# Loading and releasing an expert's up matrices by halves of the contraction

## The reference

```python
# t: 512 x 1024; w_up1, w_up3: 32 x 1024 x 512; w_down: 32 x 512 x 1024
y = jnp.zeros_like(t)
for e in range(N_EXPERTS):                      # 32
    hid = jax.nn.silu(t @ w_up1[e]) * (t @ w_up3[e])
    y = y + combine[:, e:e + 1] * (hid @ w_down[e])
```

## Time and profile before

| what | value |
|---|---|
| median of 3 runs | 1287.11 us (1286.87 to 1289.26) |
| profiled execution | 1290.17 us |
| its span, first to last instruction | 1288.4 us |
| mean granted TensorE clock | 0.937 |
| TensorE busy | 1077.4 us, 84% of the span |
| weight loads of TensorE | 558.0 us |
| VectorE / ScalarE / GpSimd busy | 348.6 / 266.6 / 193.5 us |
| read from memory | 275.56 MB |
| SP's transfer queue | 263.33 MB, 52.8% of 16 engines' span |

### The profile page before, as it was taken

How to read it: one execution, slowest core, us unless ns; L and a number is a source line. 1 busy time by engine, 2 the same in 40 slices (tenths; PEclk the granted TensorE clock), 3 DMA queues, 4 the chain that set the end, 5 groups by cost and what they waited for, 6 DMA issues and landing times.

```text
span 1288.4 us, 15070 instructions
## 1 busy us (share of the span) xinstructions
PE 1077.4 (84%) x6355; PEld 558.0 (43%) x6355; DVE 348.6 (27%) x544; ACT 266.6 (21%) x406; POOL 193.5 (15%) x238
## 2 busy tenths in 40 slices
PE   0599999979999999999899469987878888887870
PEld 0578544545556677554345323333323333332320
DVE  3722562155547211102423421000000000000004
ACT  2233340255432343113112100000000000000003
POOL 2435100033330001000100011211111111111000
PEclk9799999989999999999999679989999999988895
DMA  9413103214431002214150849999999999999945
GB/s 307 174 66 131 65 3 128 65 66 164 163 135 63 2 2 68 99 34 149 47 212 33 330 181 406 403 396 400 410 404 409 406 413 402 381 396 408 411 176 199
DMA packets 69388, 280.49 MB, mean 218 GB/s; under 512 B 8379, under 2 KB 17709, under 8 KB 61147
## 3 DMA queue, kind: packets, MB, share of 16 engines
q1 hardware_dynamic: 59232, 263.33, 52.8%
q0 software_dynamic: 5120, 8.40, 2.0%
q10 hardware_dynamic: 4986, 8.04, 1.8%
HBM read 275.56 MB, written 12.58 MB: 224 GB/s over the span
## 4 chain that ended last, share of the span: by engine, by line
PE 50%; DMA 29%; DVE 12%; SPq 5%; ACT 2%; issue 1%; POOL 0%; ACTq 0%; POOLq 0%; DVEq 0%
DMA arena<-in_w_up 23%; PE ps L1672 8%; PE ps L1392 6%; SPq L367 5%; DMA ring<-in_w_mod 5%; PE ps L1282 4%; PE ps L1630 4%; PE ps L1466 3%; PE ps L1596 2%; PE ps L1403 2%; PE ps L1295 2%; PE ps L1296 2%; PE ps L1297 2%; PE ps L1331 2%; DVE arena L877 2%; PE ps L1687 1%
## 5 line engine op out<-in xcount | busy, mean ns | idle before, releaser
L1672 PE MATMUL ps<-arena 128*64 128x512 f32 x672 | 170.9, 667 | 49.0 <-DMA arena<-in_w_up 49.0
L1204 DVE TENSOR_TENSOR arena<-arena,ps 128x256 f32<-128x256 f32 x32 | 13.5, 421 | 434.8 <-ACT arena L824 434.8
L1672 PEld LDWEIGHTS ps<-arena 128*64 128x64 f32 x672 | 58.4, 153 | 160.8 <-issue 160.8
L1392 PE MATMUL ps<-arena,ring 128*128 128x512 f32 x256 | 119.9, 606 | 0.0
L1672 PE MATMUL ps<-ring,arena 128*64 128x512 f32 x352 | 87.4, 653 | 17.5 <-DMA ring<-in_w_up 16.5
L1687 PE MATMUL ps<-arena 128*64 128x512 f32 x336 | 76.7, 598 | 11.6 <-DVE arena L1206 11.6
L824 ACT ACTIVATE arena<-ps 128x256 f32<-128x256 f32 x32 | 12.3, 383 | 309.5 <-PE ps L1672 309.5
L1392 PEld LDWEIGHTS ps<-arena,ring 128*128 128x128 f32 x256 | 45.5, 190 | 46.6 <-issue 45.1
L1672 PEld LDWEIGHTS ps<-ring,arena 128*64 128x64 f32 x352 | 30.5, 150 | 73.3 <-issue 73.3
L1282 PE MATMUL ps<-arena,ring 128*128 128x512 f32 x128 | 55.1, 592 | 0.0
L828 ACT ACTIVATE arena<-ps 128x512 f32<-128x512 f32 x32 | 19.1, 597 | 167.6 <-PE ps L1687 167.6
(11 more groups left out here) (320 smaller groups left out, 1530.2 us busy)
## 6 DMA issues: line engine op xcount, KB each, us to landing
arena<-in_w_up SPq DMA_DIRECT2D x42, 2048.0 KB, 34.5
ring<-in_w_up SPq DMA_DIRECT2D x22, 2048.0 KB, 33.5
ring<-in_w_mod SPq DMA_DIRECT2D x12, 2048.0 KB, 8.7
ring<-in_w_down SPq DMA_DIRECT2D x11, 2048.0 KB, 37.2
arena<-in_w_down SPq DMA_DIRECT2D x11, 2048.0 KB
arena<-in_w_down SPq DMA_DIRECT2D x20, 1024.0 KB, 32.3
ring<-in_w_in SPq DMA_DIRECT2D x6, 2048.0 KB, 8.0
ring<-in_w_in SPq DMA_DIRECT2D x8, 1024.0 KB, 7.9
```

Source lines behind the costliest of these rows:

```text
L1392: last = mm(ps[:, bank, :], w[:, k, P * (n % 2):P * (n % 2) + P], hT[:, k, :], start=(k == 0), stop=(k == KD - 1))
L1672: last = mm(ps[64 * hf:64 * hf + 64, UP_BANK[u], :].rearrange("p (m n) -> p m n", m=2), hgT[:, k, :], up_pair(u, k)[:, :, 256 * hf:256 * h ...
```

## The change

Every byte goes to the same place in SBUF as before, and the 32 matmuls are the same in the same order. What changes is how the bytes are grouped into transfers and when they are released:

- `load_expert(eng, u, m, e)` with m < 2 no longer loads matrix m whole. It loads half m of the contraction (the slices k = 4m to 4m+3, which are 2048 floats or 8 KB on each partition) of both matrices, as two transfers of 1 MB. Both raise `w_in_sem[u][m]`, which so counts 32 for a turn.
- `expert_up` waits for half 0 only before its first matmul, and for half 1 before the 17th. The 16th matmul raises a new semaphore, `up_half`.
- SP waits on `up_half` and loads half 0 of the expert three ahead, then waits on `up_done` and loads half 1, then as before on `down_done` and w_down. The same is done in the loop for overflowing blocks and for the last two experts.

```diff
         def load_expert(eng, u, m, e):
             if m < 2:
-                src = esrc[m][:, bass.ds(e, 1), :].rearrange("p a n -> p (a n)")
-                eng.dma_start(eset_up[u][m], src).then_inc(w_in_sem[u][m], 16)
+                for i in range(2):
+                    src = esrc[i][:, bass.ds(e, 1), 2048 * m:2048 * m + 2048].rearrange("p a n -> p (a n)")
+                    eng.dma_start(eset_up[u][i][:, 2048 * m:2048 * m + 2048], src).then_inc(w_in_sem[u][m], 16)
...
             with sp.Fori(0, LOOPED // NSET - 1) as it:
                 for u in range(NSET):
+                    sp.wait_ge(up_half, NSET * it + (u + 1))
+                    load_expert(sp, u, 0, NSET * it + (NSET + u))
                     sp.wait_ge(up_done, NSET * it + (u + 1))
-                    load_expert(sp, u, 0, NSET * it + (NSET + u))
                     load_expert(sp, u, 1, NSET * it + (NSET + u))
                     sp.wait_ge(down_done, NSET * it + (u + 1))
                     load_expert(sp, u, 2, NSET * it + (NSET + u))
...
             for u in range(E - LOOPED):
+                sp.wait_ge(up_half, NSET * again + (u + 1))
+                sp.sem_inc(register_pass, 1)
+                load_expert(sp, u, 0, LOOPED + u)
                 sp.wait_ge(up_done, NSET * again + (u + 1))
                 sp.sem_inc(register_pass, 1)
-                load_expert(sp, u, 0, LOOPED + u)
                 load_expert(sp, u, 1, LOOPED + u)
...
             def expert_up(u, it):
                 pe.wait_ge(hg_ready, NSET * it + (u + 1))
-                pe.wait_ge(w_in_sem[u][0], it * 16 + 16)
-                pe.wait_ge(w_in_sem[u][1], it * 16 + 16)
+                pe.wait_ge(w_in_sem[u][0], it * 32 + 32)
                 for k in range(KD):
+                    if k == KD // 2:
+                        last.then_inc(up_half, 1)
+                        pe.wait_ge(w_in_sem[u][1], it * 32 + 32)
                     for hf in range(2):
                         last = mm(ps[64 * hf:64 * hf + 64, UP_BANK[u], :].rearrange("p (m n) -> p m n", m=2), hgT[:, k, :],
                                   up_pair(u, k)[:, :, 256 * hf:256 * hf + 256], start=(k == 0), stop=(k == KD - 1))
                 last.then_inc(up_done, 1)
```

More of the change, by code:

```diff
@@ L287, in build @@
         w_in_sem = [[sem(f"expert_w{m}_in{u}") for m in range(3)] for u in range(NSET)]
+        up_half = sem("up_half")
         hrow_zero, idx_link, dst_link, dst_ready = sem("hrow_zero"), sem("idx_link"), sem("dst_link"), sem("dst_ready")
@@ L434, in _ @@
                         e = sp.value_load(nblk_i[0:1, bass.ds(NSET * it + 2 + u, 1)], min_val=0, max_val=E - 1)
+                        sp.wait_ge(up_half, NSET * it + (LOOPED + u + 1 - NSET))
+                        load_expert(sp, u, 0, e)
                         sp.wait_ge(up_done, NSET * it + (LOOPED + u + 1 - NSET))
-                        load_expert(sp, u, 0, e)
                         load_expert(sp, u, 1, e)
```

## The result

The changed kernel takes 1274.86 us (median of 6 runs, 1272.86 to 1280.05); the kernel before took 1288.58 us beside it (6 runs, 1286.87 to 1291.12). The ratio is 0.9897, with a 95% interval of 0.9881 to 0.9913. That is about 13.3 us faster, where 7.2 were forecast; the forecast of 1280 was 5 us too long and the time lies under its range.

The account below looks back on a forecast made before the run. Bound taken as one continuous transfer stream from first buffer release to the end; -3.43 - 5.37 + 0.14 + 1.5 = -7.2 us, from the median 1287.11 to 1279.9, so 1280; range 1276.5 to 1289 us.

Parts of the forecast that it names:

- What bounds the kernel: From first weight-buffer release to the end: one continuous stream of transfers; only earlier start, faster stream or less work behind helps.
- Start of the stream: Behind expert 0's 16th up matmul: first loads issued at about 761.8 instead of 765.2 us, gain 3.43 us.
- the bubble: Early in the stream, after the first half loads: the queue running dry would eat the 3.4 us; forecast not to happen.
- Behind the last landing: Last expert's up product: only 16 matmuls, 3.43 us instead of 8.80, stand behind the last landing, gain 5.37 us.
- The three conditions: At the last expert: first half lands in time (5.1 us ahead), TensorE is free, w_down is there.
- the cover: Last expert's w_down, landed before its down product starts at 1254.10 us: 6.1 us of cover, 5.4 used.
- The middle: Experts between the stream's ends: no gain; SP's extra issues, 0.8 us per expert, are hidden in its waits.
- the 0.14 us of the second wait: TensorE's added wait ahead of matmul 17: on the path once, at the last expert, cost 0.14 us.
- A slower stream: cost 1.5 us: Up loads in 8 KB instead of 16 KB pieces, 58 more transfers: cost 1.5 us, bounds 0 and 18.
- Larger gain: Rival: stream gets faster, small gathers and scatters coming between shorter pieces; 1270 to 1276 us, chance 0.05.

Follow-up runs that it names:

- e4: Changed kernel, but TensorE waits for both halves ahead of its first matmul; SP still releases by halves. Ratio 0.9926 to the kernel before.
- e2: Changed kernel with only the new grouping into four 1 MB transfers; both halves released and waited for together. Ratio 0.9964 to the kernel before.
- e1: The kernel before, unchanged, run again as a control. Ratio 1.0000 to the kernel before.
- e6: Kernel before with each up matrix in two transfers, partitions 0 to 63 and 64 to 127, pieces of 16 KB. Ratio 1.2751 to the kernel before.
- e5: Kernel before with its 2 MB transfers, but SP also waits for landings so less stands in the queue. Ratio 1.0025 to the kernel before.
- e10: Kernel before with each up matrix's 2 MB transfer written as two 8 KB pieces per partition, which were merged. Ratio 1.0002 to the kernel before.
- e9: Kernel before with each up matrix in two transfers that take every second partition, pieces of 16 KB. Ratio 0.9995 to the kernel before.
- e3: Changed kernel, but SP releases both halves only at the end of the up product; TensorE still waits by halves. Ratio 0.9929 to the kernel before.
- e7: Changed kernel, but SP waits for the next expert's w_down to land ahead of the first half's load. Ratio 0.9906 to the kernel before.
- e13: Kernel before with a matrix's halves apart in SBUF, so its 2 MB transfers are cut into 8 KB pieces. Ratio 0.9961 to the kernel before.
- e14: Kernel with the splitting alone, without row gathers and scatters, so not computing the whole. Ratio 0.9625 to the kernel before.
- e15: Kernel before without row gathers and scatters, unsplit 16 KB pieces, so not computing the whole. Ratio 0.9578 to the kernel before.

## Why the prediction was wrong, point by point

**What bounds the kernel** was right: a continuous stream from the first release to the end. In the two profiles its start (3.4 us), its length (5.2) and what stands behind its last landing (5.1), with the 1.7 us of chance ahead of expert 0, make 15.4 of the 15.5 us. With the sizes that are typical of all runs (3.4, some 4, and 3.4 or 5.1) they make 11 to 13 us of the 13.3 (11.2 to 15.3 by the interval).

**Start of the stream** (3.43 us): this step was right. It is 3.39 in the trace, passed on without a gap: the queue's share is 1.00 in 767 to 772, where the bubble would have been. e4 against e2: 4.9, with an uncertainty that holds 3.4.

**Behind the last landing** (5.37 us): 8.80 became 3.68, so 5.1 between the two profiles. In e1 and e2 the undivided product took 7.10 at full clock, and then the gain is 3.4. Of the eight kernels, e6 aside, that compute the whole and keep this product undivided, the profiles of two (before, e5) have 8.8 us, after some 2.5 us of idle TensorE, and six have 7.1, after 0.7 to 0.9 us, or after 2.48 us in e10. So the term has one of two values, and after some 2.5 us of idle time which one is chance; I had taken the larger as certain. The three conditions held. The halves landed 4.9 us apart (5.1 reckoned), TensorE was free, and w_down's product did not wait: its last engine had landed at 1238.3, 0.3 us ahead. That was partly luck: before, this engine had landed at 1248.6, so the cover was 5.5 us and not the 6.1 read from a window that ended at 1248. In the last product TensorE idled 1.12 and 1.22 us ahead of the halves, and the granted clock read 1.00.

**The middle** (nothing): right for SP, which is held in its issues more than before (10% of the chain on the page, where it was 5%) without harm to the stream, and the 0.14 us of the second wait are too small to see.

**The failed step: "A slower stream: cost 1.5 us".** The stream got shorter by some 4 us: 476.7 to 478.1 us in the five kernels with pieces of 16 KB that have a stream like that of before (before, e1, e5, e9, e10), 472.8 to 473.8 in the six with 8 KB (changed, e2, e3, e4, e7, e13). I had priced the smaller pieces by windows in which I took the weight queue to be alone, 430 against 421 and 404 GB/s. Only the one with 430 was: in 602 to 612 half of the bytes (2.05 of 4.04 MB) were pieces of 4 KB of ScalarE's queue, in 727 to 731 nearly a quarter (95 of 411 pieces of 4 KB). The sign was right for a stream without row transfers (e14 against e15), though the price there is 4.7 us and not 1.5, which is 10 ns for each of the 464 further pieces of an engine instead of 3.3 to 4.9; a difference of 4 GB/s cannot be read from windows of 4 us. But in the stage that counts, the row gathers and scatters of GpSimd's queue run on the same 16 engines. They drive the engines apart, by 19 us at the end; the smaller pieces bring that to 14 to 16 and keep the rate at 403 to 405, although the splitting is dearer alone. With that price of 4.7 us set against the gain, the company of the row transfers makes the splitting worth some 9 us (4.6 + 4.7, an estimate).

How much of the gain is spread and how much is rate, the engines' increments for w_down of expert 30 tell. Counted from SP's first issue, the mean of the 16 comes after 457.0 to 457.8 us in the five kernels with 16 KB and after 455.7 to 456.6 in the six with 8 KB; the last comes after 467.1 to 468.3 and 462.9 to 464.1. The average engine gains some 1 us, the slowest some 4: most of it is that the engines stay closer together. Without the rows the splitting costs the average engine 4 us (419.9 in e15, 424.1 in e14). The 1.6 us by which e7 narrowed the spread further came from the first engine, which was later (450.8 us, 448.5 in the changed kernel), and not from the last (463.7 against 463.0).

The rows for it were there. I noticed that the stream ran at 402 GB/s against 430 alone, and that at 1240 to 1244 only a quarter of the engines still worked, and used the latter only to time the halves. A share of 0.24 ahead of the last landing is a loss: the transfer that everything waits for is finished by the slowest engine, with most of the others idle. The rival "Larger gain" named the stream that gets faster beside the gathers and scatters, with 1270 to 1276 us and a chance of 0.05, wholly under the range. I wrote there that nothing in the rows asked for it; that row did.

**What stays open.** How an engine's share of time depends on the size of the other queue's pieces was not measured. The Trainium skill, "DMA: Bandwidth & Descriptors", section "Queues, rings and completion order", says that an engine takes turns between the queues it has work for, a packet at a time, where its packet is a group of some 9 to 17 descriptors and not the single piece that this profile counts. If a larger piece makes a turn longer, the other queue's small pieces wait longer for theirs. The gathers that land after 7 us instead of 9.5 agree with that, but no run here shows a turn, nor why a longer wait of the rows puts some engines behind and not others.

## What to carry to other kernels

When a long stream of large loads runs beside small transfers of another queue, price a change of the load's shape in that company and not from stretches in which the load is alone; here the sign turned. Look at the DMA share in the last microseconds ahead of the landing that everything waits for: a share that sinks slowly shows engines that have drifted apart. And split a load where its stream begins and where it ends: each edge gave what half a product lasts, and the releases between them gave nothing (stream of 473.7 us in e4, 473.3 in e2).

## What was not expected of the hardware

- Loads of 1 MB that take partitions 0 to 63 and 64 to 127 in turn ran at 222 GB/s; loads of the same number and size that take every second partition ran at 403 (e6, e9).
- Up loads in pieces of 16, 8 and 4 KB beside the row transfers: 403, 404 to 405 and 398 GB/s (4 KB in transfers of 512 KB), with the best stream at 8 KB. Without the row transfers 16 KB in 2 MB were better than 8 KB in 1 MB: 422 against 418.
- The gathers beside them land after 9.5, 7 and 6.4 us.
- Two adjacent pieces of 8 KB in one transfer are merged when they are adjacent on both sides (59232 packets), and not when they lie apart in SBUF (67424) (e10, e13). What merges them was not looked for.
- Leaving out the row transfers, 8.4 MB beside 201 MB of weights in the 32 experts, shortened the stream by 10%, from 478.1 to 431.2 us: 47 us, where 8.4 MB at the 422 GB/s of that kernel's middle would be 20, and where these packets took 2.0% of the 16 engines' span, 26 us.
